# Weight units of 1 MB loaded, rounded, subtracted and waited for in two halves

## The reference, cut to what matters

```python
proj = h @ w_in[l]                                   # first block
x = x + (gate_a * y_a + gate_f * y_f) @ w_o[l]
x = x + jnp.square(jax.nn.relu(h @ w_mlp_up[l])) @ w_mlp_down[l]
...
proj = h @ w_in                                      # second block
_, states = lax.associative_scan(combine, (a_el, bu), axis=1)   # its state-space scan
branch = jnp.einsum('bsnc,ncd->bsnd', ys, w_branch)
out = merged @ w_out
```

## Time and profile before

| | |
|---|---|
| median of 3 runs | 2271.41 us (2271.23 to 2272.01) |
| profiled execution, its own time | 2271.57 us |
| its span, first to last instruction | 2269.7 us |
| granted TensorE clock, mean | 0.998 |
| TensorE busy with matmuls | 2248.8 us, 99% of the span |
| VectorE / ScalarE / GpSimd busy | 1761.7 / 1031.8 / 313.3 us |
| rate of HBM | 208 GB/s over the span |

### The profile page before, as it was taken

The page is one execution under the profiler, slowest core; times in us unless marked ns, Lnnn a source line. Parts: engine busy times, 40 slices in busy tenths (PEclk is TensorE's granted clock), DMA queues, the critical chain, the costliest instruction groups (busy, mean ns, idle before and its releaser), DMA issues.

```text
span 2269.7 us, 30097 instructions
## 1 busy us (share of the span) xinstructions
PE 2248.8 (99%) x12660; PEld 1952.2 (86%) x12660; DVE 1761.7 (78%) x1974; ACT 1031.8 (45%) x854; POOL 313.3 (14%) x226
## 2 busy tenths in 40 slices
PE   8999999999999999999999999999999999999998
PEld 7988888888888888888888888888888888888886
DVE  6585569557697888787766789989999968458865
ACT  5555246424444445444444434544344545544442
POOL 0002101110000000000000000048878600000000
PEclk9999999999999999999999999999999999999999
DMA  7453354347755555555555556676666587666753
GB/s 277 147 193 135 137 195 176 131 145 269 273 204 200 203 202 221 202 202 202 202 203 203 204 222 227 236 252 207 209 208 218 199 306 245 214 240 251 267 197 148
DMA packets 84230, 475.19 MB, mean 209 GB/s; under 512 B 8704, under 2 KB 8832, under 8 KB 32512
## 3 DMA queue, kind: packets, MB, share of 16 engines
q1 hardware_dynamic: 84096, 473.27, 58.5%
HBM read 450.17 MB, written 23.07 MB: 208 GB/s over the span
## 4 chain that ended last, share of the span: by engine, by line
PE 94%; DVE 4%; DMA 1%; issue 1%; ACT 0%; DVEq 0%; SPq 0%; ACTq 0%
PE acc L2189 29%; PE acc L2195 29%; PE acc L2192 29%; PE banks L2336 2%; PE banks L2385 2%; DVE w_lo L1270 1%; DVE convT L1590 1%; PE banks L2464 1%; DVE padT L1317 1%; PE banks L2206 1%; DMA spilled<-stage 1%; PE banks L2453 0%; DVE a_raw L2041 0%; PE banks L2486 0%; PE banks L2504 0%
## 5 line engine op out<-in xcount | busy, mean ns | idle before, releaser
L1270 DVE TENSOR_TENSOR w_lo<-raw,w_hi 128x2048 fp32r<-128x2048 f32 x394 | 910.6, 2313 | 306.9 <-ACT w_hi L808 304.2
L808 ACT ACTIVATE w_hi<-raw 128x2048 fp32r<-128x2048 f32 x394 | 751.2, 1912 | 624.3 <-DMA raw<-in_w 619.2
L2189 PE MATMUL acc<-w_hi,a_hi 128*128 128x512 f32 x2112 | 813.1, 385 | 1.9 <-ACT a_hi L828 1.1
L2195 PE MATMUL acc<-w_hi,a_lo 128*128 128x512 f32 x2112 | 801.3, 379 | 0.0
L2192 PE MATMUL acc<-w_lo,a_hi 128*128 128x512 f32 x2112 | 801.2, 379 | 0.0
L2189 PEld LDWEIGHTS acc<-w_hi,a_hi 128*128 128x128 f32 x2112 | 399.5, 189 | 69.1 <-issue 10.2
L2195 PEld LDWEIGHTS acc<-w_hi,a_lo 128*128 128x128 f32 x2112 | 399.6, 189 | 57.0 <-DVE a_lo L1306 0.3
L2192 PEld LDWEIGHTS acc<-w_lo,a_hi 128*128 128x128 f32 x2112 | 399.8, 189 | 54.0
L2189 PE MATMUL acc<-w_hi,b_hi 128*128 128x512 f32 x928 | 352.3, 380 | 0.0
L2192 PE MATMUL acc<-w_lo,b_hi 128*128 128x512 f32 x928 | 351.7, 379 | 0.0
L2195 PE MATMUL acc<-w_hi,b_lo 128*128 128x512 f32 x928 | 351.7, 379 | 0.0
(11 more groups left out here) (351 smaller groups left out, 1679.9 us busy)
## 6 DMA issues: line engine op xcount, KB each, us to landing
raw<-in_w SPq DMA_DIRECT2D x395, 1024.0 KB, 4.8
spilled<-stage SPq DMA_DIRECT2D x72, 256.0 KB, 5.9
gate_in<-spilled SPq DMA_DIRECT2D x20, 512.0 KB, 5.8
x_rows<-in_x SPq DMA_DIRECT2D x4, 512.0 KB, 8.1
x_rows<-in_x SPq DMA_DIRECT2D x1, 2048.0 KB, 9.4
mem_rows<-in_mem SPq DMA_DIRECT2D x2, 1024.0 KB, 5.9
spilled<-stage_b SPq DMA_DIRECT2D x8, 256.0 KB, 5.7
out<-y_rows SPq DMA_DIRECT2D x3, 512.0 KB, 2.8
```

What stands on the lines that cost most here:

```text
L808: act.activation(w_hi[:, n % HIGH, :], raw[:, n % RAW, :], ACT.Copy)\
L1270: dve.tensor_tensor(w_lo[:, n % RAW, :], raw[:, n % RAW, :], w_hi[:, n % HIGH, :].bitcast(F32), ALU.subtract).then_inc(lo_split, 1)
L2189: pe.matmul(o, hi[:, tk], wh, start=first, stop=False)
L2195: ins = pe.matmul(o, lo[:, tk], wh, start=False, stop=last)
```

## The change

A unit is handled in two halves of 1024 columns of `raw`, which are K steps 0, 1 and 2, 3, just those that TensorE's part 0 and part 1 use. The load becomes two DMAs of 512 KB with a semaphore each, the rounding two ACTIVATE of 128x1024 that each wait for their half, the subtraction two TENSOR_TENSOR of 128x1024 that each wait for their rounding, and TensorE waits for `lo_split` ahead of both parts, each time for the half that it needs. The very last unit, whose parts are cut by token tile instead, waits for both halves at once. Nothing else moves, and the buffers stay the same.

```diff
--- before.py
+++ after.py
@@ -31,6 +31,7 @@
 NW = 512
 KU = 4
 UE = KU * NW
+HALVES = (slice(0, UE // 2), slice(UE // 2, UE))
 LANES = 2
 RAW = 4
 HIGH = 4
@@ -492,7 +493,7 @@
 
         act_done, dve_done, pool_done, pe_done = (sem(f"{e}_done") for e in ("act", "dve", "pool", "pe"))
         done = {"act": act_done, "dve": dve_done, "pool": pool_done, "pe": pe_done}
-        landed = [sem(f"landed{i}") for i in range(RAW)]
+        landed = [[sem(f"landed{i}_{h}") for h in range(2)] for i in range(RAW)]
         hi_split, lo_split = sem("hi_split"), sem("lo_split")
         early_hi, early_lo = sem("early_hi"), sem("early_lo")
         quarter_landed = [sem(f"quarter_landed{k}") for k in range(KU)]
@@ -635,7 +636,8 @@
 
                 if n >= RAW:
                     sp.wait_ge(pe_used, n - RAW + 1)
-                sp.dma_start(raw[:, n % RAW, :], t_in["w"][n]).then_inc(landed[n % RAW], 16)
+                for h, c in enumerate(HALVES):
+                    sp.dma_start(raw[:, n % RAW, c], t_in["w"][n][:, c]).then_inc(landed[n % RAW][h], 16)
 
             def load(dst, src, landing):
                 sp.dma_start(dst, src).then_inc(landing, 16)
@@ -802,16 +804,16 @@
 
             def split(n):
 
-                act.wait_ge(landed[n % RAW], 16 * (n // RAW + (n % RAW > 0)))
                 if n >= HIGH:
                     act.wait_ge(pe_used, n - HIGH + 1)
-                act.activation(w_hi[:, n % HIGH, :], raw[:, n % RAW, :], ACT.Copy)\
-                   .then_inc(hi_split, 1)
+                for h, c in enumerate(HALVES):
+                    act.wait_ge(landed[n % RAW][h], 16 * (n // RAW + (n % RAW > 0)))
+                    act.activation(w_hi[:, n % HIGH, c], raw[:, n % RAW, c], ACT.Copy).then_inc(hi_split, 1)
 
             def quarter(n, k):
 
                 c = slice(k * NW, (k + 1) * NW)
-                act.wait_ge(landed[n] if n else quarter_landed[k], 16)
+                act.wait_ge(landed[n][k // 2] if n else quarter_landed[k], 16)
                 act.activation(w_hi[:, n, c], raw[:, n, c], ACT.Copy).then_inc(early_hi, 1)
 
             def job(tag, j):
@@ -1266,9 +1268,10 @@
 
             def split(n):
 
-                dve.wait_ge(hi_split, n + 1 - EARLY)
-                dve.tensor_tensor(w_lo[:, n % RAW, :], raw[:, n % RAW, :], w_hi[:, n % HIGH, :].bitcast(F32),
-                                  ALU.subtract).then_inc(lo_split, 1)
+                for h, c in enumerate(HALVES):
+                    dve.wait_ge(hi_split, 2 * (n - EARLY) + h + 1)
+                    dve.tensor_tensor(w_lo[:, n % RAW, c], raw[:, n % RAW, c], w_hi[:, n % HIGH, c].bitcast(F32),
+                                      ALU.subtract).then_inc(lo_split, 1)
 
             def quarter(n, k):
 
@@ -2167,8 +2170,8 @@
                         by = CHUNKS[i - 2][3]
                         pe.wait_ge(act_emptied if by == "act" else dve_emptied,
                                    emptied(i - 2, by))
-                if part == 0 and n >= EARLY:
-                    pe.wait_ge(lo_split, n + 1 - EARLY)
+                if n >= EARLY:
+                    pe.wait_ge(lo_split, 2 * (n - EARLY) + (2 if n == UNITS - 1 else part + 1))
                 op = operand(name)
                 ks = range(part * KU // 2, (part + 1) * KU // 2)
                 order = [(k, t) for k in ks for t in range(NT)]
```

## The result

| | before | after |
|---|---|---|
| median | 2271.72 us (2270.96 to 2274.01, 16 runs) | 2275.55 us (2274.57 to 2278.39, 16 runs) |
| ratio, 95% interval | | 1.0017 (1.0010 to 1.0023) |
| profiled execution, own time (span) | 2271.57 us (2269.7) | 2274.62 us (2272.6) |

The halves cost 3.8 us. That is a loss, since the interval leaves out 1, but less than half of the 9.2 us forecast: 2275.55 us for 2280.6.

What follows compares the result with a forecast made beforehand. TensorE was taken as the bound, VectorE as full in the scan stage. 0.46 + 1.1 less 0.12 spare, 1.44 us late a period, over 7.3 periods is 10.5, less 1.3: 9.2 us, so 2280.6 us (8 in 10: 2271.7 to 2287.5).

Steps and rivals of the forecast that it cites:

- TensorE's wait: 394 waits added on TensorE, each alone on its matmul: taken as 0, bounds 0 and 32 us.
- the load and the rounding: Smaller loads, issued four units ahead, and one more ScalarE instruction a unit: both taken as 0, hidden by idle time.
- The instruction: VectorE's second subtraction instruction: +0.07 us a unit, +0.46 us in a period of seven units.
- VectorE's headroom of 0.12: Scan stage: VectorE has 39.48 us of work in 39.60, so 0.12 us to spare a period.
- the price of the boundary: Scan stage: GpSimd gets in between the subtraction's halves and holds up VectorE, +1.1 us a period, bounds 0 and +1.5.
- the early half and the slack: TensorE needs only the first half for part 0; with slack at the tightest unit, 1.3 us before TensorE waits.
- the 41 that the forecast named as its sign: Two steps of the scan stage were to take 41 us for 39.60, with VectorE full and TensorE short of it.
- free boundaries: Scan stage: two steps at 39.6 to 40.0 us would mean that the subtraction's new boundaries cost nothing.
- theory A: The loss is VectorE's added instruction, some 0.07 us a unit, in the scan stage where VectorE is full.
- B: The loss is GpSimd getting in at the new boundary of the subtraction, in the scan stage.
- The walk behind the 1.1: Scan step priced meeting by meeting, GpSimd always let in: 2.97 us for 2.2, +1.45 a period, three quarters taken.
- the first rival: Scan stage: boundaries cost nothing net, 1.2 us in all, 2272.6 us; decides below 0.45 us a period; chance 0.16.

Runs made afterwards that it cites:

- e3_one_wait: The changed kernel, but TensorE waits once a unit, ahead of part 0 and for both halves: 2276.51 us, ratio 1.0019.
- e5_whole_tight: The changed kernel, but in units 256 to 319 (scan stage) the subtraction is whole and TensorE waits once a unit: 2272.87 us, ratio 1.0005.
- e1_whole_sub: The changed kernel, with loads and roundings in halves but the subtraction and TensorE's wait whole: 2273.06 us, ratio 1.0008.
- e11_whole_load: The changed kernel, but each unit loaded by one DMA of 1 MB: 2276.34 us, ratio 1.0019.
- e4_quarters: The changed kernel, but the subtraction in four parts of 512 columns in units 256 to 319: 2286.03 us, ratio 1.0059.
- e2_only_sub: The kernel before, with only the subtraction and TensorE's waits in halves, loads and roundings whole: 2278.94 us, ratio 1.0031.
- e6_nopool_before: The kernel before, with 14 of GpSimd's 16 rotation tables left out, so old tables are used: 2271.38 us, ratio 0.9999.

## Why the forecast of the loss was more than twice too large

**Right.** The bound, the place and the sign. TensorE's wait costs nothing that can be told (e3_one_wait, e5_whole_tight), the load and the rounding nothing (e1_whole_sub, e11_whole_load), and other stages absorb the subtraction (e5_whole_tight, and 43.64 of 60 us in the light window). The instruction was taken at 0.46 us a period and measured 0.45. VectorE's headroom of 0.12 holds too: its period is 40.17 us (1670.45 to 1710.62) for 39.48 (1629.25 to 1668.73), 0.69 more, and TensorE's 0.57 more.

**The term that was mis-sized** is the price of the boundary: taken at +1.1 us a period, measured 0.69 - 0.45 = 0.24. With it the sum is 7.3 x (0.45 + 0.24 - 0.12) = 4.2, less the 1.3 that the early half and the slack give, so 2.9 us. The stage shows 3.3, the spans 2.9, the medians 3.8. Two steps take 40.17 us, between the 41 that the forecast named as its sign and the 39.6 to 40.0 that it set for free boundaries. So the added instruction (theory A) is two thirds of VectorE's loss, and the boundary (B) one third.

A smaller term was off the other way. The early half and the slack were taken to give 1.3 us; 7.3 x 0.57 - 3.3 makes it 0.9. The tightest unit early in the stage is not 277, with its 0.31 us of slack, but 270, with 0.20, and without the early half (e3_one_wait) the stage loses 0.75 more. From the start of unit 277, where TensorE is 0.88 us early, to that of 319, where it is 2.51 late, it loses 3.4 us in six periods.

The walk behind the 1.1 went wrong in two places, both to be seen in the timelines above.

- *A length with GpSimd in it was taken as the bare one.* In the step from 1670.45 each meeting of the walk came as priced: 2.78 for 2.28 in the first subtraction, 3.39 for 2.27 in the second, L1934 at 1.64 for 2.30, 3.37 for 2.64 in the third. But the walk gave the second scans only their 0.8 back, down to 1.95 us. That 1.95 itself had GpSimd in it; bare, the pair takes 1.26. So 0.7 us more came back, and the whole step lasts 21.35 us (1670.45 to 1691.80) for 21.06 (1629.25 to 1650.31), that is 0.29: four added instructions of 0.07 and nothing for boundaries.
- *The step in which VectorE keeps the way is as frequent as the other.* In the step from 1691.80, and so in every second one, GpSimd gets in at none of the first two middles nor ahead of L1934. It lasts 18.82 us (1691.80 to 1710.62) for 18.42 (1650.31 to 1668.73), 0.40 more: three added instructions and 0.2 for boundaries. Here, too, much of what is lost comes back late in the step: the third subtraction takes 3.13 us for 2.65 and its scans 2.72 for 2.07, but L1945 then takes 1.23 where L1942 took 2.11. The walk was made for the first kind and scaled by three quarters.

The lower end of that term was given as 0, and the first rival as "boundaries cost nothing net", which decides below 0.45 us a period. By that condition this rival, at a chance of 0.16, came true in its mechanism; the time, 2275.55 us, lies between its 2272.6 and the forecast's own 2276.5 to 2285, as the boundaries don't cost quite nothing. What GpSimd takes at a new boundary it gives back later in the step. That it gives back nearly all is shown for the order of this kernel's steps; that it must, because GpSimd's work is fixed and a meeting is only moved, is argued and not shown. e4_quarters speaks against a rule of no price: there the new boundaries cost 0.3 us a period.

The Trainium skill (SBUF — State Buffer, the section on who interferes with whom) was read as speaking against the change. The traces agree with what it says, that one engine stands for the whole of the other's instruction (L1934 at 1.64 us for 1.21, behind a product of GpSimd; L1226 at 4.57 us for 1.28, behind VectorE). What I drew from it, that more boundaries mean as much more time lost, they don't bear out.

**Left open.** Why `w_lo` is 0.86 us less ahead of TensorE in e2_only_sub than in the changed kernel already at unit 236, before the collision. A whole rounding is as much longer than a half one (1.91 us for 1.06), but that it is the cause is argued and not shown. Why the `gate_in` of units 76 to 80 comes late in some profiles, and why the granted clock falls behind one wait of 2.4 us and not behind another of 2.6. What decides whether GpSimd or VectorE goes first at a boundary is open too.

## What to carry to other kernels

Cutting work finer pays only where someone waits for the first piece. Here TensorE had waited 0.2 us in all for a `w_lo`, so there was next to nothing to gain, and the cut cost time in the one stage where the engine that was cut had 0.12 us to spare in 39.6.

To price contention in a queue, take every operation's bare length from where the other engine is idle, for all of them, and sum a whole period over each kind of step. A length that has contention in it makes what comes back look too small.

## What was not expected of the hardware

- A scan of 256 columns on VectorE takes 677 ns where GpSimd is idle and 1108 to 1208 ns on the mean beside it. GpSimd's tables lengthen VectorE's two steps from 33.0 us of work (mean of four windows of e6_nopool_before) to 39.5.
- A TENSOR_SCALAR of 128x32 stood for a whole MEMSET of GpSimd (1.66 and 1.83 us for 0.18), while in the changed kernel three TENSOR_TENSOR of the same size started beside the same MEMSET (1439.95 to 1441.77), at 0.19 us each:

```profile
1440.09 0.19 DVE L1800 TENSOR_TENSOR ssm_t<-ssm_t 128x32 f32<-128x32 f32 x1
1440.31 0.19 DVE L1802 TENSOR_TENSOR ssm_t<-ssm_t 128x32 f32<-128x32 f32 x1
1440.54 0.19 DVE L1804 TENSOR_TENSOR ssm_t<-ssm_t 128x32 f32<-128x32 f32 x1
```

- Who goes first at a boundary is no matter of luck here. L1934 takes 1.64 us and 1.21 us by turns in all 13 steps from 1558.30 to 1799.30, in step with the four and three subtractions that a step has by turns.
